# Split rows kept in DRAM for the passes of the first matrix, and a weight sum moved to VectorE

## What is computed

```python
h = layer_norm(DEEPNORM_ALPHA * h + attn_out, ln1_g[l], ln1_b[l])
u = jnp.square(jax.nn.relu(h @ w_ff1[l] + b_ff1[l]))
ffn_out = u @ w_ff2[l] + b_ff2[l]
h = layer_norm(DEEPNORM_ALPHA * h + ffn_out, ln2_g[l], ln2_b[l])
```

## Time and profile before

| | |
|---|---|
| median of 3 runs | 3284.99 us |
| the runs | 3275.3, 3284.99, 3285.01 us |
| profiled execution | 3277.12 us |
| its span | 3274.3 us |
| mean granted TensorE clock | 0.987 |
| start of the passes, end of the last unit | 2557.5, 3158.3 us |

### The profile page before, as it was taken

How to read it: one execution, slowest core, us unless ns; L and a number is a source line. 1 busy time by engine, 2 the same in 40 slices (tenths; PEclk the granted TensorE clock), 3 DMA queues, 4 the chain that set the end, 5 groups by cost and what they waited for, 6 DMA issues and landing times.

```text
span 3274.3 us, 43156 instructions
## 1 busy us (share of the span) xinstructions
PE 3139.0 (96%) x16490; PEld 2685.6 (82%) x16490; DVE 2184.2 (67%) x3203; ACT 1281.8 (39%) x2127; POOL 1236.3 (38%) x941
## 2 busy tenths in 40 slices
PE   7999999998999999999999999999999889999998
PEld 7889999998988888789776788888887668777777
DVE  6779998456277899965545034443453898989965
ACT  5452221453155422225424245444522644444431
POOL 2317442113223383321231343221433566676731
PEclk9999999999999999999999999999999999999999
DMA  6101222214311112220141411111243323131211
GB/s 162 39 23 50 72 82 87 51 27 157 124 59 33 39 46 77 91 76 31 44 152 52 170 55 44 38 46 62 101 135 135 109 72 132 62 124 70 95 60 65
DMA packets 253745, 257.83 MB, mean 79 GB/s; under 512 B 37207, under 2 KB 208902, under 8 KB 249958
## 3 DMA queue, kind: packets, MB, share of 16 engines
q1 hardware_dynamic: 225862, 151.74, 15.6%
q0 software_dynamic: 21920, 82.13, 6.7%
q10 hardware_dynamic: 5760, 21.22, 1.6%
HBM read 197.33 MB, written 59.50 MB: 78 GB/s over the span
## 4 chain that ended last, share of the span: by engine, by line
PE 71%; DVE 11%; issue 6%; POOL 6%; ACT 5%; DMA 1%; DVEq 0%; ACTq 0%; POOLq 0%
PE big L901 41%; PE big L1443 9%; PE small L1050 4%; PE small L1443 3%; PE big L1013 2%; PE small L964 2%; PE big L1029 2%; DVE rows_split L3091 2%; POOL wsp L2245 2%; PE small L901 1%; POOL tm L2365 1%; DVE tm L3018 1%; PE big L953 1%; PE big L935 1%; DVE hid L3266 1%
## 5 line engine op out<-in xcount | busy, mean ns | idle before, releaser
L901 PE MATMUL big<-H,wsp 128*128 128x348 f32 (+3 forms) x7488 | 1506.0, 359 | 28.1 <-DVE H L2800 11.8
L901 PEld LDWEIGHTS big<-H,wsp 128*128 128x128 f32 (+1 forms) x7488 | 1292.8, 188 | 202.1 <-issue 23.1
L2245 POOL TENSOR_TENSOR wsp<-raw,wsp 128x1024 fp32r<-128x1024 f32 (+2 forms) x182 | 388.1, 2132 | 1016.1 <-ACT wsp L1550 1010.3
L1443 PE MATMUL big<-rows_split,wring 128*128 128x512 f32 x1788 | 440.0, 403 | 30.5 <-DVE rows_split L3091 27.0
L1443 PEld LDWEIGHTS big<-rows_split,wring 128*128 128x128 f32 x1788 | 340.8, 192 | 122.7 <-DVE rows_split L3091 18.0
L2245 POOL TENSOR_TENSOR wring<-wr,wring 128x512 fp32r<-128x512 f32 x196 | 312.7, 1602 | 182.1 <-ACT wring L1673 181.6
L2997 DVE MAX8 top<-SC 128x8 f32<-128x528 f32 (+4 forms) x320 | 306.0, 956 | 0.0
L3001 DVE MATCH_REPLACE8 SC<-top,SC 128x528 f32<-128x528 f32 (+4 forms) x320 | 303.3, 948 | 0.0
L1550 ACT ACTIVATE wsp<-raw 128x1024 fp32r<-128x1024 f32 (+2 forms) x182 | 170.6, 937 | 202.8 <-DVE X L3038 104.5
L1673 ACT ACTIVATE wring<-wr 128x512 fp32r<-128x512 f32 x196 | 121.8, 627 | 187.2 <-PE big L1443 111.8
L3091 DVE TENSOR_TENSOR rows_split<-stage,rows_split 128x512 fp32r<-128x512 f32 x148 | 170.2, 1206 | 36.9 <-ACT rows_split L1997 36.8
(11 more groups left out here) (394 smaller groups left out, 4673.4 us busy)
## 6 DMA issues: line engine op xcount, KB each, us to landing
raw<-in_w_in SPq DMA_DIRECT2D x108, 512.0 KB, 3.7
wr<-in_w_ff SPq DMA_DIRECT2D x28, 1024.0 KB, 6.4
stage<-combo_scratch SPq DMA_DIRECT2D x21, 1024.0 KB, 4.8
raw<-in_w_out SPq DMA_DIRECT2D x24, 512.0 KB, 5.0
gate_b_scratch<-tm POOLq DMA_DIRECT2D x16, 522.0 KB, 3.0
gate_a_scratch<-tm ACTq DMA_DIRECT2D x16, 522.0 KB, 2.8
tm<-gate_a_scratch POOLq DMA_DIRECT2D x16, 522.0 KB, 3.9
tm<-gate_b_scratch POOLq DMA_DIRECT2D x16, 522.0 KB, 4.7
```

Source lines behind the costliest of these rows:

```text
L901: mm = pe.matmul(dst(o, width), w[wp][:, k, 0:cols], last_rows(xp, k, t0, width) if rhs is None else rhs(xp, k)[:, t0:t0 + width], start=( ...
L1443: mm = pe.matmul(unit_bank(n), w[:, wp, k, :], x[:, xp, k, :], start=(j in FIRST_STEPS and k == 0 and term == 0), stop=(k == 3 and term == ...
L2245: pool.tensor_tensor(dst, src, hi.bitcast(F32), ALU.subtract).then_inc(*S.inc(name, *key))
```

## The change

1. The rows of the even passes are stored split. In pass 0 SyncE stores `row_split` of every step (`split_out`, 2 MB: hi and lo), and in passes 2, 4 and 6 loads it for each step right into `row_split` (`rows_in`). ScalarE and VectorE do no `rows_hi` and `rows_lo` there. In pass 0 (and step 8) `rows_hi` waits until the buffer's store has ended.
2. `rows_hi` and `rows_lo` take two halves of 128 x 1024 in place of four pieces, from step 3 on.
3. Relu and square of steps 4 to 6 of the even passes go from one VectorE instruction to two of ScalarE (`act_square`).
4. Step 0's block of passes 3 and 5 is added to `kept_v` by VectorE from the bank, and `add_v` is done once, 12 adds beside the plain products at the end.
5. Sum 2 of the odd passes is made by VectorE beside units 24 to 27 of the pass before. In pass 0 GpSimd's sums 2 and 4 move from the normalization and units 0 to 3 to behind unit 2 and to units 12 to 15; sums 1 and 3 go behind the load of the h_old of their m, m = 4 and 5. GpSimd's sum 4 of odd passes moves to units 8 to 11.
6. VectorE in odd passes does `rows_lo` and the post of unit 0 first, then T3, and T2 after the post of unit 2. SyncE issues A12 at j = 2 in passes 2, 4 and 6 (else j = 3), A21 at j = 3, A22 at j = 4.

```diff
+            def split_out(s):
+                sp.wait_ge(*S.at("rows_lo", s, 3))
+                sp.dma_start(split_d[s], row_split[s % 2][:].bitcast(F32).rearrange("p h k n -> p (h k n)"))\
+                    .then_inc(*S.dma(*split_stored(s)))
+
+            def rows_in(s):
+                if s < STEPS * PASSES and rows_from_store(s):
+                    sp.wait_ge(*S.at("unit", 4 * (s - 1) - 1))
+                    sp.wait_ge(*S.at(*split_stored(s % STEPS)))
+                    sp.dma_start(row_split[s % 2][:].bitcast(F32).rearrange("p h k n -> p (h k n)"), split_d[s % STEPS])\
+                        .then_inc(*S.dma(f"rows_in{s % 2}", s))
...
+                    if q == 0:
+                        split_out(j)
+                    rows_in(STEPS * q + j + 1)
                     if q + 1 < PASSES:
                         if j == 1:
                             quad_in(q + 1, "A11", ("weight_split", UNITS * (q - 1) + 27) if q else ("projected", ("out2", 7)))
-                        elif j == 3:
+                        elif j == (3 if q % 2 or q == 0 else 2):
                             quad_in(q + 1, "A12", ("weight_split", first + 11), ("sums_made", q, 4, 3))
+                        if j == 3:
+                            quad_in(q + 1, "A21", ("weight_split", first + 15))
                         elif j == 4:
-                            quad_in(q + 1, "A21", ("weight_split", first + 15))
-                        elif j == 5:
                             quad_in(q + 1, "A22", ("weight_split", first + 19))
...
-                        pe.wait_ge(*S.at("rows_lo", s, k))
+                        pe.wait_ge(*S.at(*rows_there(s, k)))
...
+            def act_square(n):
+
+                q, j, i = unit_of(n)
+                if q % 2 or j < 4:
+                    return
+                a_half, t = ((1, 0), (1, 1), (0, 1))[j - 4]
+                x = hid[(a_half, t)][:, i, :]
+                act.wait_ge(*S.at("bank_read", n))
+                act.activation(x, x, ACT.Relu).then_inc(*S.inc("hidden_relu", n))
+                act.wait_ge(*S.at("hidden_relu", n))
+                act.activation(x, x, ACT.Square).then_inc(*S.inc("hidden_ready_act", q, a_half, t, i))
...
                 act.wait_ge(*S.at("unit", 4 * (s - 1) - 1))
-                act.activation(row_split[s % 2][:, 0, k, :], src[:, k, :], ACT.Copy).then_inc(*S.inc("rows_hi", s, k))
+                if s < STEPS + 2:
+                    act.wait_ge(*S.at(*split_stored(s - 2)))
+                act.activation(row_split[s % 2][:, 0, first:end, :], src[:, first:end, :], ACT.Copy)\
+                    .then_inc(*S.inc("rows_hi", s, end - 1))
...
                 if n > 5:
                     unit_hi(n + RING)
+                act_square(n)
                 if n == LAST_UNIT - 1:
                     weight_hi(act, before_passes)
...
+                if m in (4, 5):
+                    for i in range(4):
+                        sums(0, (1, 3)[m - 4], i)
                 if m < 6:
                     after(("out2", m))
-                if m in (3, 4):
-                    for i in range(4):
-                        sums(0, (1, 3)[m - 3], i)
...
                 unit_lo(n + RING)
+                if n == 0:
+                    pool.wait_ge(*S.at("unit", 2))
+                    for i in range(4):
+                        sums(0, 2, i)
...
-                if n < 4:
-                    sums(0, 4, n)
-                if 23 <= r < 27:
+                if 12 <= n < 16:
+                    sums(0, 4, n - 12)
+                if q % 2 and 8 <= r < 12:
+                    sums(q, 4, r - 8)
+                if q % 2 and 23 <= r < 27:
                     sums(q + 1, 2, r - 23)
...
+                if q % 2 and j == 0:
+                    v = kept_v[:, i // 2, i % 2 * BANK:(i % 2 + 1) * BANK]
+                    wait(("bank_read_act", UNITS + i) if q == 3 else ("bank_read", n - 2 * UNITS))
+                    dve.tensor_tensor(v, v, bank, ALU.add).then_inc(*read)
+                    return
...
                 dve.scalar_tensor_tensor(x, bank, b_ff1[:, b:b + 1], x, ALU.add, ALU.add).then_inc(*read)
-                wait(("bank_read", n))
-                dve.scalar_tensor_tensor(x, x, 0.0, x, ALU.max, ALU.mult)\
-                    .then_inc(*S.inc("hidden_ready", q, a_half, 0 if j == 4 else 1, i))
...
-                if q % 2 and (j, i) == (0, 0):
-                    made_rows(q, 3)
-                if q % 2 and (j, i) == (0, 1):
-                    made_rows(q, 2)
                 if i == 0 and s > 1:
-                    for k in range(4):
-                        rows_lo(s + 1, k)
-                if q % 2 and 1 <= j <= 3:
-                    add_v(q, j - 1, i)
+                    for first, end in row_parts(s + 1):
+                        rows_lo(s + 1, first, end)
                 post(n)
+                if q % 2 and j == 0 and i in (0, 2):
+                    made_rows(q, 3 - i // 2)
...
+                if q % 2 == 0 and n % UNITS in range(24, 28):
+                    early_sums(q + 1, 2, n % UNITS - 24)
```

More of the change, by code:

```diff
@@ L440, in step_rows, with split_stored, rows_from_store, row_parts @@
                 return x_quad(b_half, t), []
-            return hid[(b_half, t)], [("hidden_ready_act" if (b_half, t) == (0, 0) else "hidden_ready", q - 1, b_half, t, 3)]
+            return hid[(b_half, t)], [("hidden_ready_act", q - 1, b_half, t, 3)]
         def sum_made(q, which, i):
-            return ("sums_made_dve" if q and which in (1, 3) else "sums_made", q, which, i)
-        def combo_stored(j):
-            return (f"combo_out{j if 2 <= j <= 5 else 0}", j)
+            return ("sums_made_dve" if q and (which in (1, 3) or which == 2 and q % 2) else "sums_made", q, which, i)
+        def split_stored(s):
+            return (f"split_out{s % 2}", s)
+        def rows_from_store(s):
+            return s // STEPS % 2 == 0 and s >= STEPS
+        def row_parts(s):
+            return [(k, k + 1) for k in range(4)] if s <= 2 else [(0, 2), (2, 4)]
+        def rows_there(s, k):
+            if rows_from_store(s):
+                return (f"rows_in{s % 2}", s)
+            return ("rows_lo", s, next(end for _, end in row_parts(s) if end > k) - 1)
         def unit_bank(n):
@@ L463, in emptied @@
             q, j, i = unit_of(n)
-            by_act = j == 0 or (j == 1 and q % 2 == 0)
+            by_act = (j == 0 and q not in (3, 5)) or (j == 1 and q % 2 == 0)
             return ("bank_read_act" if by_act else "bank_read", n)
@@ L1968, in act_post @@
                 bank = unit_bank(n)
-                if j == 0:
+                if j == 0 and q not in (3, 5):
                     act.wait_ge(*S.at("unit", n))
@@ L2201, in _ @@
                 if i == 0 and n > 4:
-                    for k in range(4):
-                        rows_hi(STEPS * q + j + 1, k)
+                    for first, end in row_parts(STEPS * q + j + 1):
+                        rows_hi(STEPS * q + j + 1, first, end)
                 if q == 0 and j == 6:
                     for c in (2 * i, 2 * i + 1):
-                        for w in (combo_stored(6), ("rows_lo", 6, 3)):
-                            act.wait_ge(*S.at(*w))
+                        act.wait_ge(*S.at("rows_lo", 6, 3))
                         act.activation(X[:, c, 0:SEQ], X[:, c, 0:SEQ], ACT.Identity, scale=ALPHA, bias=b_o[:, 1, c:c + 1])\
@@ L2447, in ln @@
                         unit_lo(n)
-                        sums(0, 2, n)
+                    pool.wait_ge(*S.at("unit", 0))
                     unit_lo(4)
@@ L3139, in ln @@
                     if k > 1:
[L3140 removed]
+                        rows_lo(2, k - 2, k - 1)
                 first_rows(3)
[L3142 to L3143 removed]
+                rows_lo(2, 2, 3)
+                rows_lo(2, 3, 4)
             ln(0, residual)
```

103 lines of the change are left out of this document (41 added, 62 removed).

## The result

| | before | after |
|---|---|---|
| median (runs) | 3282.72 us (4) | 3258.57 us (4) |
| lowest and highest | 3275.3, 3285.01 | 3255.67, 3261.05 |
| profiled execution, its span | 3277.12, 3274.3 | 3258.81, 3256.9 |
| mean granted TensorE clock | 0.987 | 0.988 |
| start of the passes, end of the last unit | 2557.5, 3158.3 | 2551.9, 3135.8 |

A forecast was written before the change was run, and what follows sets the result against it. PE, busy 96%, was taken as the bound, losing 28.5 us at odd passes' boundaries to VectorE's late rows. Terms -6.2 + 1.4 - 7.1 - 6.2 + 2.6 = -15.5 gave 3261.6 profiled; half of 7.9 added gave 3266, range 3246 to 3285.

The forecast's parts named there:

- Even passes: Passes 2, 4, 6: removed rows work gains 0 directly; 2 MB loads land in 7.5 us of 11.2, cost 0.
- Start: Before the passes: PE's waits of 3.80 us for weights and 2.43 us for the residual go, -6.2 us.
- Passes 3 and 5: Boundary stalls of 7.65 and 6.74 us at the second steps shrink to 0.5 each: gains 7.1 and 6.2 us.
- Two later waits: PE waits marked "issue" in passes 3 (1.19 us) and 5 (its like), counted as staying.
- End of pass 0: Pass 0 and boundary to pass 1: new stalls of 15.5 us replace the old 14.15, +1.4, between -10 and +8.
- X: The end of step 3 of pass 0, 2622.52 before; the forecast's times there count from it.
- four further MB at 2.7 put A22 at X+20.1: End of pass 0: A22 lands behind queued transfers; VectorE, wanting it at X+9 or so, stands for 11 us.
- ScalarE is the bound: After the stall at step 6 of pass 0, ScalarE has 26.1 us of work in the next step: 6.6 us lost.
- Tail: Plain product: its weights come behind a post and a pair, +2.1 us, and 0.5 for the clock: +2.6.
- all boundary waits go: First rival, chance 0.17: the 15.5 us at the boundary to pass 1 become 2; -29 us, 3252.
- The others: Boundary waits stay (0.20, 3278), or slower (0.08): even-pass rows land after their step's 11.2 us, 3289 to 3325, say 3300.
- second rival: Boundary waits stay where they are, 6 us left in passes 3 and 5 too: -3 us, 3278; chance 0.20.

The follow-up runs named there:

- e9: Kernel after with pass 0's weight sums back at their old places on GpSimd (1 and 3 ahead of later loads, 2 in normalization, 4 at units 0 to 3): 3251.25 us.
- e4: Kernel after with sum 2 of the odd passes back on GpSimd, beside units 23 to 26 of the pass before: 3256.56 us.
- e5: Kernel after with T3 and T2 of the odd passes again ahead of rows_lo and the posts in VectorE's list: 3258.15 us.
- e6: Kernel after with relu and square of the even passes again one VectorE instruction, not two of ScalarE: 3251.61 us.
- e10: Kernel after with the even passes' rows stored unsplit again, loaded to stage, rounded and subtracted for each pass, in halves: 3255.10 us.
- e1: Kernel after with A12 of pass 1 issued behind A22, not ahead of A21, in pass 0 alone: 3242.34 us.
- e3: e1 with the scalings of X one per unit over units 24 to 31, and the first plain product's weights made two units earlier, behind unit 192: 3240.67 us.
- e11: Kernel after with the edits of e10 and e6 together, unsplit rows and VectorE's relu and square both back: 3256.27 us.

## Why the prediction was right, and where it wasn't

The forecast of 3266 in 3246 to 3285 held (3258.57), and so did the sign. The total came out closer than its terms: in the pair of profiles they were off by +0.7 (start), -1.3 (end of pass 0), -4.4 (passes 3 and 5), +2.5 (tail) and +0.6 (pass 0's first steps), -1.9 together. That these cancel is luck. By steps:

- **Even passes: cost 0.** Right. The 2 MB load was put at 7.5 us and took 8.0. Two further MB ahead take the rows from 8.0 to 13.6 us, 2.8 each; 2.7 had been used.
- **Start: -6.2.** -5.5 in the pair of profiles. The two waits that were named are what goes and, in e9, what comes back (6.1 us). But unit 0 starts anywhere from 2548.4 to 2554.4 in eleven profiles with the new start (mean 2551.1), and at 2557.5, 2559.5 and 2563.0 with the old one. The 3 us between 6.1 and the means' 8.9 are not explained.
- **Passes 3 and 5: -13.3, with 0.5 us left in each.** The two stalls of the earlier trace rows went in full, -14.4. The failed step is "Two later waits, ... are "issue", of no engine; I count them as staying": they went as well, some 3.2 us. They were VectorE's all the time. Its timeline of before ends the post of the unit whose bank PE needs (2868.90 + 0.67) 0.1 us before PE's row starts at 2869.67:

```profile
2868.90 0.67 DVE L3252 TENSOR_TENSOR X<-X,big 128x512 f32<-128x512 f32 x1
```

  The chain itself was reckoned too slow. The rows of the second step were put 1.2 us ahead of their due time; they ended at 2828.67 where PE asks at 2833.36, 4.7 ahead:

```profile
2826.31 2.36 DVE L3113 TENSOR_TENSOR rows_split<-hid,rows_split 128x1024 fp32r<-128x1024 f32 x2 [1.72 <-ACT rows_split L2018]
```

  A half takes 1.18 us there, where 2.0 and, for the two of step 1, 1.7 had been reckoned: 2.7 of the 3.5 us. The sums were priced rightly (the five took 5.15 us by their rows, in place of 5.0). The 1.7 is a slip: with the forecast's own 2.0 the second half of step 1 ends at 21.8, 0.6 ahead.
- **Why they went.** The prediction added up many savings in one chain, and they do clear it, with 4.7 us to spare. It did not say that they overlap: taken back one at a time (e4, e5, e6, e10) none of them returns a microsecond to passes 3 and 5, and two of the largest together return 2.5 of 9. The 4.7 us fit this (T3's 3.2 us, put back ahead in e5, are less).
- **End of pass 0: +1.4.** +0.1, by two errors that cancel. "so A12 goes at X+4.5" and "four further MB at 2.7 put A22 at X+20.1": with X = 2617.49 A12 went at X+8.2, and A22 had landed at X+25.7. Only the last of sum 4's pieces had been counted; the three before it had pushed back the splits between them (3.36 and 2.28 us, not 1.3). (By its own terms, X+2.7 and 1.5, the forecast should have said X+4.2.) And from A12's issue to A22's landing it took 17.5 us, not 15.6: the view by stretches has 354 GB/s from 2626 to 2643, with the DMA engines 96% busy, 3.0 us per MB and not 2.7. Whether the store of step 5, issued behind A22, has a part in it no run shows. VectorE stood 16.3 us in place of 11, and 10.1 us were lost ahead of step 6, in place of 5.9. On the other side stands "ScalarE is the bound ... 26.1 us": the same instructions took 23.4 (2649.88 to 2673.24). The smaller part of this is the prices (a pair took 1.25 us, not 1.3). The larger is that durations had been added, while in a gapless queue the next row can start before the last has ended (0.63 us long, 0.53 to 0.66 to the next start). PE also used up 1.85 us by itself: from 2649.95 on, after 9.9 us without work, step 6 took 13.05 us, at a mean granted clock of 0.85 in the view by stretches, so in part at the lower level of 1.2 GHz. So 1.6 us were lost ahead of step 8, and 6.6 had been reckoned. The place and the cause of the stall were right, as e1 shows by removing it.
- **Tail: +2.6.** +5.1. The wait grew as reckoned (+1.7 against 2.1), but 3.4 us follow it in place of 0.5. Up to the last matmul of the plain products it is 1.4 us more (99.7 from the first against 98.4 before), the slow first rows behind the wait (0.77 us for one matmul, 0.40 in e3), at a granted clock of 0.51, the lower level, from 3138.96 to 3142.03. 2.0 more come after it, in the last normalization; why is open. It doesn't hang on the wait: e9 and e10 have the same wait and only 0.3 and 0.6 us of it.
- **The sum** was 3261.6 for the profiled execution, which took 3258.8. The half of 7.9 us added for the median was not called for: the median of after is 0.2 us from its profile.

Of the rivals, "all boundary waits go" did not happen in the change; e1, where VectorE no longer waits for A22, shows that it would have with A12 elsewhere. The others did not happen. The second rival's -3 is a slip: with 6 us left in each of passes 3 and 5 its terms give -4.6.

## What to carry over

Before an engine's work is cut, ask in which stretch it is late, and by how much: 204 us of VectorE's work went, and what had made PE wait were 9 us at each of two boundaries, of which the small edits (e11) repair 6 and more. When a transfer in the DMA queue has to wait for a sum or a split, issue the transfers that an engine will soon need ahead of it, not behind: A12's one place in the list was worth 14 us, over half of what the whole change gains. And of a change made of many edits, take each back by itself: here neither of the two in its name was worth anything by itself, with the rest in place.

## What the runs showed of the hardware

- A wait marked "issue" can be another engine's: before, VectorE's post of the bank ends at 2869.57 and the matmul starts at 2869.67 (1.19 us), and in e11 it is 2831.52 and 2831.61 (1.71 us). By `bank_free` that matmul waits for just this post, and where the profile does name the releaser, at step 6 of the kernel after, the post ends 0.1 us ahead too (2649.84, 2649.95).

```profile
2831.61 3.04 PE L1457 MATMUL big<-rows_split,wring 128*128 128x512 f32 x12 [1.71 <-issue]
```

- VectorE's and GpSimd's two-input instructions are slower side by side. A half of `rows_lo` is 1.18 us with GpSimd idle (2.36 for two at 2657.27 in the kernel after), and 2.3 when it is full (4.60 for two at 2836.50); GpSimd's split of 128 x 512 is 1.29 us by itself, and up to 3.36 here.
- ScalarE's rows of 128 x 512 in a gapless queue start 0.53 us apart where nothing depends on the last, and 0.66 where the next reads its result, at 0.63 us each in the profile. The Trainium skill (Perfetto Trace Analysis, Summary: the profiler window per engine type) has the reason: the reported window runs to the acknowledgement of the write. Adding durations counts that part again for each row: between 2649.88 and 2673.24 the rows add up to 25.0 us where 23.4 passed, 1.6 of the 2.7 us between 26.1 and 23.4.
